# Conditioning sums of two segments moved from TensorE to GpSimd

## The chip, the cores and the metric

One core of one Trainium2 chip runs the kernel. The metric is the device time of one execution in microseconds, as the median of several. A core has five engines with queues of their own: TensorE (PE), VectorE (DVE), ScalarE (ACT), GpSimd (POOL) and SyncE (SP, which here issues DMAs). They are ordered against each other by semaphores alone.

## The reference, cut to what matters

Two decoder layers over 256 tokens of width 1024, the first with native sparse attention, the second with latent attention, each followed by a SwiGLU network. Each sub-layer is modulated by a conditioning vector:

```python
cond = jax.nn.silu(c)
for i in range(DEPTH):
    mod = cond @ ada_w[i] + ada_b[i]
    sh_m, sc_m, g_m, sh_f, sc_f, g_f = [t[:, None, :] for t in jnp.split(mod, 6, axis=-1)]
    hm = _rms(x, norm_mix[i]) * (1.0 + sc_m) + sh_m
    ...
    x = x + g_m * y.astype(x.dtype)
    hf = _rms(x, norm_ffn[i]) * (1.0 + sc_f) + sh_f
    x = x + g_f * _swiglu(hf, ffn_w_in[i], ffn_w_out[i])
```

Everything is float32. The twelve parts of `mod` (two layers, six each) are the segments 0 to 11. Segments 3 and 4 are `sh_f` and `sc_f` of the first layer. A segment is a product of the 1024 conditioning values with a 1024x1024 block of `ada_w`, plus a bias.

## The kernel before

**Weights.** All weights go through a ring. SP loads 1 MB at a time into `raw`; ACT copies half of it, a "slot" of 128x1024, rounded, into `w_hi` (line 776); DVE writes the rest, `raw - w_hi`, into `w_lo` (line 1121). PE multiplies each slot in three products (high by high, low by high, high by low; lines 1808 to 1810) into PSUM tensors `lin`. `w_hi` and `w_lo` have four slots, so ACT and DVE prepare a slot when PE has used the one four before it. A plain slot is 12 products of 512 columns, a slot of a compression unit 12 of 256.

**The first mixer.** After the first two input units (until about 59 us) PE goes through `U_KVW`, `U_QA`, the gates, the first compression `U_CMPK`, `U_QB` and the second compression `U_CMPV`, four slots each but for the gates. Between them stand transposes of what DVE has made from earlier units. DVE's program, an order written out by hand, is for this stretch: `w_lo` of the next slots; `normed_keys(0)` (sums of squares, a chain of ten small operations for reciprocal roots, two scalings L1390); `blocks(0)` (L1405); `normed_keys(1)`; `blocks_low` (`a_lo`, L1411); `blocks(1)`; `normed_queries(0)` (L1422, the same chain, L1426); `blocks_low`; `ada_biases(3)`; and, after the scaled copies of the queries, `normed_queries(1)`, `ada_biases(4)` and the compressed key. PE needs `a_lo` before each compression, the scaled keys before their transposes, and the second `normed_queries` before the last ones.

**Conditioning segments.** Segments 0 and 1 are done in the first 50 us. The weights of the others come as chunks of 128 rows by 1024 columns (512 KB), eight to a segment, through `ada_ring`, which has three places; POOL issues these loads (line 613) when a chunk three before is used. For segments 2 and 5 to 11 DVE adds each chunk, times its conditioning value, into `acc` (line 1205), and PE sums `acc` over the partitions at the end (`reduce_columns`, `reduce_row`). For segments 3 and 4 PE multiplies each chunk itself: after each slot of `U_KVW`, `U_QA`, `U_CMPK` and `U_QB` stands one `ada_chunk`, four fp32 matmuls of 32 by 256 (eight records in the profile) into `sc`. DVE then adds a bias into `ada_rows` (line 1214), PE turns that (`ada_turned`, line 1961), and `ada_columns` copies the result out.

**POOL** otherwise makes constants, issues small loads, zeroes and biases `acc` (line 683), adds steps of the first attention's output (line 703) and rotates the queries of the second (lines 440 to 447).

Of the kernel before, what the change touches and what calls it, by code (L numbers as in the profile page):

```python
# [17 lines left out]
F32 = mybir.dt.float32  # L18
# [49 lines left out]
BLOCKS = D // AQ  # L68

# [99 lines left out]
def rows_by_pe(seg):  # L169

    return sum(s not in VEC_SEGS for s in ADA_ORDER[:ADA_ORDER.index(seg)])


def chunks_by_pe(a):

    return sum(seg_at(n // KD) not in VEC_SEGS for n in range(EARLY * KD, a))
# [16 lines left out]
def trunk(nc, x_in, c_in, positions, ada_w, ada_b, norm_mix, norm_ffn, ffn_w_in, ffn_w_out,  # L193
# [4 lines left out]
    with ctx:  # L198
# [11 lines left out]
        ada_rows = sb("ada_rows", [P, 3, AQ], F32)  # L210
        ada_bias = sb("ada_bias", [P, 2, AQ], F32)
# [58 lines left out]
        with nsa:  # L270
# [12 lines left out]
            cstat = sb("cstat", [P, 3, H], F32, nsa)  # L283

# [58 lines left out]
        bias_zero = sem("bias_zero")  # L343
        bias_landed = [sem(f"bias_landed{n}") for n in range(2)]
        acc_bias = sem("acc_bias")
        ada_used = sem("ada_used")
        ada_biased = sem("ada_biased")
# [254 lines left out]
        def _(pool):  # L602
# [12 lines left out]
            def issue_bias(seg):  # L615
                layer, s6 = divmod(seg, 6)
                n = rows_by_pe(seg)
                if n >= 2:

                    pool.wait_ge(ada_biased, n - 1)  # L620
                for j in range(4):
                    c0 = s6 * D + AQ * j
                    pool.dma_start(ada_bias[32 * j:32 * j + 1, n % 2, :],
                                   ada_b[layer:layer + 1, c0:c0 + AQ]).then_inc(bias_landed[n % 2], 16)

# [3 lines left out]
            nc.gpsimd.memset(ada_bias[:], 0.0).then_inc(bias_zero, 1)  # L629
# [26 lines left out]
            pool.wait_ge(bias_zero, 1)  # L656
# [6 lines left out]
            def issue_next(a):  # L663

                if a + ARING < NSEG * KD:
                    if seg_at(a // KD) in VEC_SEGS:
                        pool.wait_ge(acc_summed, chunks_by_dve(a + 1))
                    else:
                        pool.wait_ge(ada_used, chunks_by_pe(a + 1))
                    issue(a + ARING)  # L670
# [18 lines left out]
            for seg in (3, 4):  # L689
                issue_bias(seg)  # L690
                supply(seg)
# [414 lines left out]
        def _(dve):  # L1106
# [102 lines left out]
            def ada_biases(seg):  # L1209

                n = rows_by_pe(seg)
                dve.wait_ge(ada_used, chunks_by_pe((place_of(seg) + 1) * KD))
                dve.wait_ge(bias_landed[n % 2], 64 * (n // 2 + 1))
                nc.vector.tensor_tensor(ada_rows[:, seg % 3, :], sc[place_of(seg) % 2][:, 0:AQ], ada_bias[:, n % 2, :],
                                        ALU.add).then_inc(ada_biased, 1)

            def ada_columns(seg):
                dve.wait_ge(ada_red, ada_at(seg))
                if seg in VEC_SEGS:
                    nc.vector.tensor_copy(ada_cols[:, seg, :], sc[seg % 2][:, 0:KD]).then_inc(ada_out, 1)  # L1220
                else:
                    nc.vector.tensor_copy(ada_cols[:, seg, :].rearrange("p (j h) -> p j h", h=2),
                                          sc[place_of(seg) % 2][:, 256:512].rearrange(
                                              "p (h j r) -> p j h r", h=2, r=32)[:, :, :, 0]).then_inc(ada_out, 1)
# [227 lines left out]
            ada_biases(3)  # L1452
# [7 lines left out]
            ada_biases(4)  # L1460
# [342 lines left out]
        def _(pe):  # L1803
# [53 lines left out]
            def unit(unit, s0, slots, n, lhs, wait_st=None, chunk_after=()):  # L1857
# [4 lines left out]
                for q, kts in enumerate(slots):  # L1862
# [12 lines left out]
                    if q in chunk_after:  # L1875
                        ada_chunk()
# [53 lines left out]
            def rows_product(seg, kt, chunk):  # L1930

                for j in range(4):
# [544 lines left out]
```

## Time and profile before

| | |
|---|---|
| median of 3 runs | 737.58 us (736.84 to 737.87) |
| the profiled execution | 737.94 us, span 736.1 us |
| PE busy | 699.7 us (95%) |
| DVE busy | 525.1 us (71%) |
| ACT busy | 373.4 us (51%) |
| POOL busy | 98.2 us (13%) |
| mean granted TensorE clock | 0.995 of full speed |

The span runs from the first to the last instruction; the execution's own time is 1.8 us longer. Busy times of PE count pipelined matmuls that overlap, so its pace is better read from the distance between their starts. Times of POOL are rougher than those of the others. "Idle before" is the time an engine stood still ahead of an instruction, with what released it.

### The profile page before, as it was taken

Reading aid. Unit: us, or ns where it says so; the run is one execution under the profiler, and the core shown is the slowest. Engines: PE = TensorE matmul, PEld = TensorE weight load, DVE = VectorE, ACT = ScalarE, POOL = GpSimd, SP = SyncE. Lnnn points to the kernel's source line nnn. Section 1 sums busy time; section 2 is a strip of 40 time slices with the busy share of each in tenths; the row PEclk is TensorE's granted clock in tenths of the full one; section 3 lists DMA queues with packets and bytes.
Section 4 is the critical chain, followed back from the end, with each engine's and each line's share of the span. In section 5 each row is a group of like instructions: output and inputs, shape, how many; then the busy total and the mean of one; then the engine's idle time right before and its main releaser. Section 6 shows DMA issues by size and latency. Waiting matters only on the chain. (4 is left out here: it accounts for less than half of the span.)

```text
span 736.1 us, 10780 instructions
## 1 busy us (share of the span) xinstructions
PE 699.7 (95%) x3903; PEld 575.5 (78%) x3903; DVE 525.1 (71%) x981; ACT 373.4 (51%) x696; POOL 98.2 (13%) x182
## 2 busy tenths in 40 slices
PE   3699999999989999999999999889999999999997
PEld 1577768888878888878878897778888888878886
DVE  3346687898888889887786578977767755554444
ACT  3244566577447444444333379676465444444341
POOL 7020212022110111221111100600001000000000
PEclk9999999999999999999999999999999999999999
DMA  8997996032248999997798372601538766554521
GB/s 289 351 371 187 372 369 228 2 116 86 90 170 262 334 326 354 321 342 273 265 341 289 94 211 66 228 1 59 172 111 276 230 189 193 171 173 171 204 83 57
DMA packets 93742, 155.09 MB, mean 211 GB/s; under 512 B 5979, under 2 KB 68064, under 8 KB 93696
## 3 DMA queue, kind: packets, MB, share of 16 engines
q1 hardware_dynamic: 80768, 111.24, 46.0%
q0 software_dynamic: 12928, 43.24, 17.3%
q8 instruction: 28, 0.46, 0.3%
q14 instruction: 18, 0.15, 0.1%
HBM read 151.32 MB, written 1.05 MB: 207 GB/s over the span
## 5 line engine op out<-in xcount | busy, mean ns | idle before, releaser
L776 ACT ACTIVATE w_hi<-raw 128x1024 fp32r<-128x1024 f32 (+3 forms) x198 | 201.5, 1024 | 263.2 <-PE lin L1810 238.3
L1121 DVE TENSOR_TENSOR w_lo<-raw,w_hi 128x1024 fp32r<-128x1024 f32 (+3 forms) x198 | 233.2, 1185 | 119.3 <-ACT w_hi L776 118.8
L1808 PE MATMUL lin<-w_hi,st_hi 128*128 128x512 f32 (+2 forms) x568 | 226.6, 399 | 2.3 <-DVE w_lo L1121 2.0
L1810 PE MATMUL lin<-w_hi,st_lo 128*128 128x512 f32 (+2 forms) x568 | 218.9, 385 | 0.0
L1809 PE MATMUL lin<-w_lo,st_hi 128*128 128x512 f32 (+2 forms) x568 | 218.6, 385 | 0.0
L1808 PEld LDWEIGHTS lin<-w_hi,st_hi 128*128 128x128 f32 x568 | 107.3, 189 | 28.1 <-issue 6.1
L1810 PEld LDWEIGHTS lin<-w_hi,st_lo 128*128 128x128 f32 x568 | 107.3, 189 | 21.3
L1809 PEld LDWEIGHTS lin<-w_lo,st_hi 128*128 128x128 f32 x568 | 107.6, 189 | 19.3 <-issue 0.7
L613 POOL DMA_DIRECT2D ada_ring<-in_ada_w_dram x80 | 42.7, 534 | 324.8 <-DVE acc L1205 238.7
L1205 DVE SCALAR_TENSOR_TENSOR acc<-ada_ring,cond_b,acc 128x1024 f32<-128x1024 f32 x64 | 81.8, 1279 | 3.3 <-DMA ada_ring<-in_ada_w_dram 3.1
L1808 PE MATMUL lin<-w_hi,hid_hi 128*128 128x512 f32 x176 | 70.1, 398 | 0.0
L1810 PE MATMUL lin<-w_hi,hid_lo 128*128 128x512 f32 x176 | 69.0, 392 | 0.0
L1809 PE MATMUL lin<-w_lo,hid_hi 128*128 128x512 f32 x176 | 68.5, 389 | 0.0
L1810 PEld LDWEIGHTS lin<-w_hi,hid_lo 128*128 128x128 f32 x176 | 33.0, 188 | 7.7
L1809 PEld LDWEIGHTS lin<-w_lo,hid_hi 128*128 128x128 f32 x176 | 33.1, 188 | 7.3 <-issue 0.2
L1808 PEld LDWEIGHTS lin<-w_hi,hid_hi 128*128 128x128 f32 x176 | 33.1, 188 | 6.8 <-issue 0.2
L848 ACT ACTIVATE z<-z,nmax 128x128 f32<-128x128 f32 x64 | 28.4, 445 | 11.6 <-DVE nmax L1279 11.6
L813 ACT ACTIVATE tfull<-tp,ada_cols,scale_cols 128x256 f32<-128x256 f32 x32 | 16.6, 558 | 13.9 <-issue 6.1
L1172 DVE TENSOR_TENSOR st_lo<-tfull,st_hi 128x512 fp32r<-128x512 f32 (+1 forms) x22 | 13.3, 607 | 12.8 <-ACT st_hi L816 12.6
L794 ACT ACTIVATE scratch<-x 128x512 f32<-128x512 f32 x16 | 10.0, 626 | 23.1 <-DVE x L1256 20.1
L1833 PE MATMUL tp<-ident,scratch 128*128 128x128 f32 x65 | 11.3, 299 | 10.9 <-DVE st_lo L1172 8.1
L1248 DVE TENSOR_TENSOR scratch<-lin,gate_rows 128x512 f32<-128x512 f32 x16 | 11.0, 687 | 11.3 <-PE lin L1810 11.3
(257 smaller groups left out, 858.1 us busy)
## 6 DMA issues: line engine op xcount, KB each, us to landing
raw<-in_ffn_w_in_dram SPq DMA_DIRECT2D x88, 512.0 KB, 5.2
ada_ring<-in_ada_w_dram POOLq DMA_DIRECT2D x80, 512.0 KB, 6.3
raw<-in_ffn_w_out_dram SPq DMA_DIRECT2D x22, 1024.0 KB, 6.1
raw<-in_nsa_w_in_dram SPq DMA_DIRECT2D x10, 1024.0 KB, 12.6
ada_first<-in_ada_w_dram SPq DMA_DIRECT2D x8, 1024.0 KB, 13.1
raw<-in_nsa_cmp_w_dram SPq DMA_DIRECT2D x4, 1024.0 KB, 9.9
raw<-in_nsa_w_out_dram SPq DMA_DIRECT2D x4, 1024.0 KB, 8.6
raw<-in_mla_w_out_dram SPq DMA_DIRECT2D x4, 1024.0 KB, 5.1
```

The source lines that it names most:

```text
L613: pool.dma_start(ada_ring[:, n % ARING, :], ada_source(a)).then_inc(ada_landed[n % ARING], 16)
L776: nc.scalar.activation(part_of(w_hi, s), raw_part(s), ACT.Copy).then_inc(hi_ready, 1)
L813: ins = nc.scalar.activation(dst, src, ACT.Identity, scale=scale[:, k:k + 1], bias=shift[:, k:k + 1])
L848: e = nc.scalar.activation(prob_b[:, n % 3, c0:c0 + w], prob_b[:, n % 3, c0:c0 + w], ACT.Exp, bias=nmax[:, n % 4, t:t + 1], scale=-1.0, ac ...
L1121: nc.vector.tensor_tensor(part_of(w_lo, s), raw_part(s), part_of(w_hi, s).bitcast(F32), ALU.subtract).then_inc(lo_ready, 1)
L1172: nc.vector.tensor_tensor(st_lo[:, k0:k0 + nk, :], tfull[:, m % 2, 0:nk * S].rearrange("p (k s) -> p k s", k=nk), st_hi[:, k0:k0 + nk, :]. ...
L1205: nc.vector.scalar_tensor_tensor(total, ada_ring[:, n % ARING, :], cond_b[:, kt, 0:1], total, ALU.mult, ALU.add).then_inc(acc_summed, 1)
L1248: ins = nc.vector.tensor_tensor(tmp, lin[2 * (unit % 2) + t][:], gate_rows[:, row, 512 * n:512 * n + 512], ALU.mult)
L1808: nc.tensor.matmul(bank, a_h, w_h, start=first, stop=False)
L1809: nc.tensor.matmul(bank, a_h, w_l, start=False, stop=False)
L1810: return nc.tensor.matmul(bank, a_l, w_h, start=False, stop=last)
L1833: ins = nc.tensor.transpose(tp[batch % 2][0:rows, n * P:(n + 1) * P], src, ident[:])
```

## The change

POOL gets two sums of its own, `shift_sum` and `scale_sum` (128x1024 each). At the start of its program it zeroes them and loads the bias into their first row. When the first chunks have landed it goes through the 16 chunks of segments 3 and 4: it multiplies the chunk in place by its conditioning value, waits for that, adds it to the sum, and waits for that before it issues the load of the chunk three further on. PE no longer has `ada_chunk` between its slots. Where `ada_turned` stood it now runs `reduce_columns` for both segments, which waits for POOL's sums and makes eight one-column products of each. DVE's two `ada_biases` go; `ada_columns` copies from the reduced columns. `ada_rows` shrinks, `ada_bias` and its loads go, and PE waits for the small loads explicitly in `compressed`.

```diff
 BLOCKS = D // AQ
+POOL_SEGS = (3, 4)
...
         ada_ring = sb("ada_ring", [P, ARING, D], F32)
-        ada_rows = sb("ada_rows", [P, 3, AQ], F32)
-        ada_bias = sb("ada_bias", [P, 2, AQ], F32)
+        scale_sum = sb("scale_sum", [P, D], F32)
+        ada_rows = sb("ada_rows", [P, 2, AQ], F32)
         x = sb("x", [P, T, D], F32)
...
             cstat = sb("cstat", [P, 3, H], F32, nsa)
+            shift_sum = sb("shift_sum", [P, D], F32, nsa)
+        pool_sums = {POOL_SEGS[0]: shift_sum, POOL_SEGS[1]: scale_sum}
...
-            def issue_bias(seg):
-                layer, s6 = divmod(seg, 6)
-                n = rows_by_pe(seg)
-                if n >= 2:
-
-                    pool.wait_ge(ada_biased, n - 1)
-                for j in range(4):
-                    c0 = s6 * D + AQ * j
-                    pool.dma_start(ada_bias[32 * j:32 * j + 1, n % 2, :],
-                                   ada_b[layer:layer + 1, c0:c0 + AQ]).then_inc(bias_landed[n % 2], 16)
-
             link(nc.gpsimd.memset(ident[:], 0.0))
             nc.gpsimd.affine_select(out=ident[:], in_=ident[:], compare_op=ALU.not_equal, fill=1.0, base=0,
                                     pattern=[[-1, P]], channel_multiplier=1).then_inc(ident_ready, 1)
-            nc.gpsimd.memset(ada_bias[:], 0.0).then_inc(bias_zero, 1)
+            for seg in POOL_SEGS:
+                link(nc.gpsimd.memset(pool_sums[seg][:], 0.0))
+                pool.dma_start(pool_sums[seg][0:1, :], ada_b[0:1, seg * D:(seg + 1) * D]).then_inc(sums_biased, 16)
             for n in range(ROT // 2):
...
                     pool.dma_start(dst, src).then_inc(small_in, 16)
-            pool.wait_ge(bias_zero, 1)
             pool.wait_ge(landed[2], 16)
...
                     else:
-                        pool.wait_ge(ada_used, chunks_by_pe(a + 1))
+                        pool.wait_ge(pool_summed, chunks_by_pool(a + 1))
                     issue(a + ARING)
...
-            for seg in (3, 4):
-                issue_bias(seg)
-                supply(seg)
+            def chunk_added(a):
+
+                place, kt = divmod(a, KD)
+                n = a - EARLY * KD
+                chunk = ada_ring[:, n % ARING, :]
+                total = pool_sums[seg_at(place)][:]
+                pool.wait_ge(ada_landed[n % ARING], 16 * (n // ARING + 1))
+                nc.gpsimd.tensor_scalar(chunk, chunk, cond_b[:, kt, 0:1], None, ALU.mult).then_inc(chunk_scaled, 1)
+                pool.wait_ge(chunk_scaled, n + 1)
+                if n > 0:
+                    pool.wait_ge(pool_summed, n)
+                nc.gpsimd.tensor_tensor(total, total, chunk, ALU.add).then_inc(pool_summed, 1)
+                issue_next(a)
+
+            pool.wait_ge(cond_ready, 1)
+            pool.wait_ge(sums_biased, 16 * len(POOL_SEGS))
+            for seg in POOL_SEGS:
+                for kt in range(KD):
+                    chunk_added(place_of(seg) * KD + kt)
...
-            def ada_biases(seg):
-
-                n = rows_by_pe(seg)
-                dve.wait_ge(ada_used, chunks_by_pe((place_of(seg) + 1) * KD))
-                dve.wait_ge(bias_landed[n % 2], 64 * (n // 2 + 1))
-                nc.vector.tensor_tensor(ada_rows[:, seg % 3, :], sc[place_of(seg) % 2][:, 0:AQ], ada_bias[:, n % 2, :],
-                                        ALU.add).then_inc(ada_biased, 1)
-
             def ada_columns(seg):
                 dve.wait_ge(ada_red, ada_at(seg))
-                if seg in VEC_SEGS:
-                    nc.vector.tensor_copy(ada_cols[:, seg, :], sc[seg % 2][:, 0:KD]).then_inc(ada_out, 1)
-                else:
-                    nc.vector.tensor_copy(ada_cols[:, seg, :].rearrange("p (j h) -> p j h", h=2),
-                                          sc[place_of(seg) % 2][:, 256:512].rearrange(
-                                              "p (h j r) -> p j h r", h=2, r=32)[:, :, :, 0]).then_inc(ada_out, 1)
+                nc.vector.tensor_copy(ada_cols[:, seg, :], sc[seg % 2][:, 0:KD]).then_inc(ada_out, 1)
...
             blocks_low()
-            ada_biases(3)
             low_to(CMPV0 + 3)
...
             normed_queries(1)
-            ada_biases(4)
...
                     ins.then_inc(slot_used, 1)
-                    if q in chunk_after:
-                        ada_chunk()
...
-            def rows_product(seg, kt, chunk):
-
-                for j in range(4):
-                    ins = nc.tensor.matmul(sc[place_of(seg) % 2][32 * j:32 * j + 32, 0:AQ], cond_b[:, kt, :],
-                                           chunk[:, AQ * j:AQ * j + AQ], start=(kt == 0), stop=(kt == KD - 1))
-                return ins
-
-            next_chunk = [EARLY * KD]
-
-            def ada_chunk():
-
-                a = next_chunk[0]
-                place, kt = divmod(a, KD)
-                seg = seg_at(place)
-                n = a - EARLY * KD
-                if kt == 0:
-
-                    if place == EARLY:
-                        pe.wait_ge(vec_ready, 1)
-                    else:
-                        pe.wait_ge(ada_biased, rows_by_pe(seg_at(place - 1)))
-                pe.wait_ge(ada_landed[n % ARING], 16 * (n // ARING + 1))
-                rows_product(seg, kt, ada_ring[:, n % ARING, :]).then_inc(ada_used, 1)
-                next_chunk[0] += 1
-                while next_chunk[0] < NSEG * KD and seg_at(next_chunk[0] // KD) in VEC_SEGS:
-                    next_chunk[0] += KD
-
-            def ada_turned(seg):
-
-                pe.wait_ge(ada_biased, rows_by_pe(seg) + 1)
-                for h in range(2):
-                    ins = nc.tensor.transpose(sc[place_of(seg) % 2][:, 256 + h * P:256 + (h + 1) * P],
-                                              ada_rows[:, seg % 3, h * P:(h + 1) * P], ident[:])
-                ins.then_inc(ada_red, 1)
-
             def wait_acc(seg):
...
-                wait_acc(seg)
-                total = acc[:, VEC_SEGS.index(seg) % 4, :]
+                if seg in POOL_SEGS:
+                    pe.wait_ge(pool_summed, KD * (POOL_SEGS.index(seg) + 1))
+                    total = pool_sums[seg][:]
+                else:
+                    wait_acc(seg)
+                    total = acc[:, VEC_SEGS.index(seg) % 4, :]
                 for k in range(KD):
...
-            unit(U_KVW, KVW0, FOUR, 512, stationary, latent_keys, EACH)
+            unit(U_KVW, KVW0, FOUR, 512, stationary, latent_keys)
...
+                pe.wait_ge(small_in, N_SMALL)
                 pe.wait_ge(*emptied(hidden_batch))
...
             transposed_keys(0)
-            unit(U_QA, QA0, FOUR, 512, stationary, None, EACH)
+            unit(U_QA, QA0, FOUR, 512, stationary)
             transposed_keys(1)
...
                     ins.then_inc(slot_used, 1)
-            compress(0, U_CMPK, CMPK0, None, EACH)
+            compress(0, U_CMPK, CMPK0)
             wait_tp(T_G)
             pe.wait_ge(unit_empty_act, U_GATE + 1)
             for t in range(T):
                 ins = nc.tensor.transpose(tp[T_G % 2][:, t * NG:(t + 1) * NG], gates_t[:, t * P:(t + 1) * P],
                                           ident[0:NG, 0:NG])
             ins.then_inc(tp_filled, 1)
-            unit(U_QB, QB0, FOUR, 512, stationary, None, EACH)
+            unit(U_QB, QB0, FOUR, 512, stationary)
             transposed_queries(0, T_QA)
...
             transposed_queries(1, T_QB)
-            ada_turned(3)
-            ada_turned(4)
+            reduce_columns(3)
+            reduce_columns(4)
             transposed_hidden(1, T_SCV)
```

## Rows read from the trace of the kernel before

**Rows 1.** The page's first part: busy time and share of each engine
```profile
PE 699.7 (95%) x3903; PEld 575.5 (78%) x3903; DVE 525.1 (71%) x981; ACT 373.4 (51%) x696; POOL 98.2 (13%) x182
```

**Rows 2.** Busy time by stretch: length, busy by engine, granted clock, DMA share, GB/s
```profile
55.00:124.20 69.20, 68.36 (x456) 50.95 (x454) 51.04 (x100) 39.46 (x55) 10.66 (x21) 1.00 0.92 305
55.00:111.40 56.40, 55.56 (x358) 40.24 (x357) 42.14 (x83) 31.94 (x44) 9.39 (x18) 1.00 0.93 310
```

**Rows 3.** Groups of DVE instructions by line and shape, 55 (last row: 50) to 124.1
```profile
L1121 DVE TENSOR_TENSOR w_lo<-raw,w_hi 128x1024 fp32r<-128x1024 f32 x20 | 23.9, 1217 | 11.7 <-ACT w_hi L776 11.6
L1411 DVE TENSOR_TENSOR a_lo<-scratch,a_hi 128x2048 fp32r<-128x2048 f32 x2 | 4.6, 2284 | 0.0
L1405 DVE TENSOR_TENSOR scratch<-z,vec_cols 128x120 f32<-128x120 f32 x16 | 4.5, 355 | 0.0
L1390 DVE TENSOR_TENSOR kdup_o<-proj,stat 128x512 f32<-128x512 f32 x4 | 2.6, 688 | 0.1
L1426 DVE TENSOR_TENSOR proj<-proj,stat 128x1024 f32<-128x1024 f32 x2 | 2.4, 1224 | 0.1
...
L1144 DVE TENSOR_TENSOR stat<-stat 128x16 f32<-128x16 f32 x2 | 0.4, 176 | 0.1
```

**Rows 4.** Timeline of PE between two slots (start us, us, instruction)
```profile
66.14 0.39 PE L1810 MATMUL lin<-w_hi,st_lo 128*128 128x512 f32 x1
...
67.36 0.39 PE L1809 MATMUL lin<-w_lo,st_hi 128*128 128x512 f32 x1
67.59 0.39 PE L1810 MATMUL lin<-w_hi,st_lo 128*128 128x512 f32 x1
```

**Rows 5.** Groups of PE instructions by line and shape, 59 to 126: the chunks
```profile
L1933 PE MATMUL sc<-ada_ring,cond_b 128*32 128x256 f32 x128 | 10.2, 391 | 0.8 <-DMA ada_ring<-in_ada_w_dram 0.8
```

**Rows 6.** Timeline of PE, at the old turning and at a reduction elsewhere
```profile
125.26 0.60 PE L1961 MATMUL sc<-ident,ada_rows 128*128 128x128 f32 x4
...
336.66 1.84 PE L1975 MATMUL sc<-ones,acc 128*128 128x1 f32 x16
338.36 0.48 PE L1808 MATMUL lin<-w_hi,st_hi 128*128 128x512 f32 x1
```

**Rows 7.** Groups of POOL instructions by line and shape, whole span
```profile
L703 POOL TENSOR_TENSOR kdup_o<-kdup_o,scratch 128x512 f32<-128x512 f32 x7 | 8.9, 1274 | 41.5 <-DVE scratch L1549 41.5
L683 POOL MEMSET acc<- 128x1024 f32 x8 | 7.7, 966 | 37.7 <-PE lin L1999 31.0 <-PE lin L1810 6.5
```

**Rows 8.** Timeline of DVE and POOL, 463 to 473
```profile
463.54 2.42 DVE L1121 TENSOR_TENSOR w_lo<-raw,w_hi 128x384 fp32r<-128x384 f32 x3
465.89 2.55 DVE L1723 TENSOR_TENSOR k_tok<-k_tok,stat 128x2048 f32<-128x2048 f32 x1
...
466.38 2.38 POOL L447 TENSOR_TENSOR q_tok<-scratch 128x128 f32<-128x128 f32 x1
...
472.44 0.46 POOL L447 TENSOR_TENSOR q_tok<-scratch 128x128 f32<-128x128 f32 x1
```

**Rows 9.** Timeline of POOL, first chunk loads and a memset's follower
```profile
41.97 1.64 POOL L613 DMA_DIRECT2D ada_ring<-in_ada_w_dram  x3 [26.39 <-DMA raw<-in_nsa_w_in_dram]
...
125.24 0.50 POOL L686 DMA_DIRECT2D acc<-in_ada_b_dram  x1 [0.29 <-POOL acc L683]
```

**Rows 10.** Timeline of DVE and POOL, 150 and 186 to 187
```profile
150.41 0.16 DVE L1542 SCALAR_TENSOR_TENSOR coef<-sums,gates 128x8 f32<-128x8 f32 x1
...
185.90 1.28 POOL L703 TENSOR_TENSOR kdup_o<-kdup_o,scratch 128x512 f32<-128x512 f32 x1 [3.98 <-DVE scratch L1549]
186.27 0.42 DVE L1572 TENSOR_TENSOR st_lo<-tp,st_hi 128x256 fp32r<-128x256 f32 x1 [0.18 <-ACT st_hi L834]
...
186.61 0.60 DVE L1542 SCALAR_TENSOR_TENSOR coef<-sums,gates 128x8 f32<-128x8 f32 x1
```

**Rows 11.** Busy time by stretch around 37 us, columns as in rows 2
```profile
34.00:37.30 3.30, 0.93 (x6) 0.86 (x6) 2.95 (x5) 2.41 (x4) 0.00 (x0) 0.92 1.10 356
37.40:40.80 3.40, 3.40 (x11) 2.66 (x10) 0.62 (x1) 0.00 (x0) 0.00 (x0) 0.59 1.03 408
```

More of the change, by code:

```diff
@@ L166, in seg_at, with chunks_by_pool @@
     return ADA_ORDER[place - EARLY]
[L169 to L176, printed above, removed]
+def chunks_by_pool(a):
+    return sum(seg_at(n // KD) in POOL_SEGS for n in range(EARLY * KD, a))
 def chunks_by_dve(a):
@@ L342, in trunk @@
         ident_ready = sem("ident_ready")
-        bias_zero = sem("bias_zero")
-        bias_landed = [sem(f"bias_landed{n}") for n in range(2)]
+        sums_biased = sem("sums_biased")
         acc_bias = sem("acc_bias")
-        ada_used = sem("ada_used")
-        ada_biased = sem("ada_biased")
+        chunk_scaled = sem("chunk_scaled")
+        pool_summed = sem("pool_summed")
         acc_summed = sem("acc_summed")
@@ L1855, in last_unit, with unit @@
                         ins.then_inc(part_done, 1)
-            def unit(unit, s0, slots, n, lhs, wait_st=None, chunk_after=()):
+            def unit(unit, s0, slots, n, lhs, wait_st=None):
                 wait_unit(unit)
@@ L2174, in _, with compress @@
             KT16 = [[0, 1, 2, 3], [4, 5, 6, 7], [8, 9, 10, 11], [12, 13, 14, 15]]
-            def compress(b, u, s0, among=None, chunk_after=()):
+            def compress(b, u, s0, among=None):
                 pe.wait_ge(a_ready, b + 1)
-                unit(u, s0, KT16, CH, lambda k: [(a_hi[:, k, :], a_lo[:, k, :])], among, chunk_after)
-            EACH = range(4)
+                unit(u, s0, KT16, CH, lambda k: [(a_hi[:, k, :], a_lo[:, k, :])], among)
             pe.wait_ge(consts, 1)
```

## The prediction

> **What bounds the kernel now.** I read the page's engine totals first. TensorE (PE) is busy for 95% of the span, VectorE (DVE) for 71%, GpSimd (POOL) for 13% [rows 1]. The change touches 55 to 126 us, so I cut that out next: from 55.0 to 124.2 us PE is busy for 68.36 of 69.20 us at full granted clock, and DVE for 51.04 [rows 2]. PE sets the pace here. DVE has 18 us of slack, most of it waits for ScalarE's `w_hi` (11.6 us) [rows 3]. The slack is uneven: from 55.0 to 111.4 DVE is busy for 42.14 of 56.40 us, and in this part it must finish all that PE's last compression unit needs. So two questions decide: what PE gets back, and whether DVE stays inside its slack once POOL computes beside it.
>
> **What PE gets back.** PE's timeline shows one slot's end and its chunk [rows 4]. The last weight product of a slot starts at 66.14, the second product of the next slot at 67.36, 1.22 us later, with the chunk and one product between them. The usual step is 0.23 (67.36 to 67.59), so two of them would have taken 0.46. A chunk costs PE 0.76 us; 128 records in eights are 16 chunks [rows 5], 12.2 us. PE's only wait for a chunk, 0.8 us [rows 5], lies where DVE will decide. Added to PE: the two transposes of `ada_turned`, 0.60 us for both segments, become two `reduce_columns`, each from 336.66 to 338.36 when it stands elsewhere, 1.70 us [rows 6]. So 3.4 less 0.6, +2.8 us, and nothing hides it: it stands in PE's queue ahead of filler matmuls and the transpose of the compressed key. If PE alone decided, the sum would be -12.2 + 2.8 = -9.4 us.
>
> **What POOL must do.** 16 times: a 128x1024 multiply, a wait on it, a 128x1024 add, a wait, the issue of the next chunk. A POOL add of 128x512 takes 1274 ns [rows 7], one of 128x128 takes 0.46 us undisturbed [rows 8]. That slope (0.81 us for 384 columns) gives 2.35 us for 1024; twice the 128x512 gives 2.55 as upper bound, 2.2 is the lower one if part of the small one's time is its strides. I take 2.33. No POOL multiply of one tensor is in the trace. From below stands a memset of the same size, 0.97 us [rows 7], which reads nothing; from above the add, 2.4. The multiply has one stream in and one out, the memset one out, the add two in over one read path; so it is nearest to the memset. I take 1.2 us and keep 1.0 and 2.4. From a POOL memset to the instruction that waits for it pass 0.29 us, and a DMA issue takes 0.50 to 0.55 [rows 9]: two waits and the issue are 1.1 us. Undisturbed, a chunk takes 1.2 + 2.33 + 1.1 = 4.6 us. The first three are issued from 41.97 [rows 9]; with 6 to 8 us to land POOL starts near 50 and would end at 50 + 16 x 4.6 = 124. PE, 12.2 us earlier than its 125.26 [rows 6], wants the second sum at 113. So even undisturbed the gain is nearly used up.
>
> The Trainium skill (GPSIMD Engine Reference, "When to use GPSIMD") calls one-input work on GpSimd roughly line rate. As an estimate from that page the multiply would be near 0.95 us instead of 1.2 and the total some 4 us lower; no multiply in the trace decides it.
>
> **What POOL does to DVE.** This is the larger term. At 463 to 469 us both engines work from SBUF [rows 8]. A POOL add that takes 0.46 us at 472.44 took 2.38 from 466.38 to 468.76: it ran only when DVE's product of two SBUF tensors had ended at 468.44. Three `w_lo` of 384 columns, some 0.5 us each by the 1217 ns for 1024 [rows 3], took 2.42 among POOL's adds. A DVE operation of 0.16 us at 150.41 took 0.60 at 186.61 and ended at 187.21, within 0.03 us of the end of POOL's 1.28 us add [rows 10]. Right before it DVE's `st_lo`, with one input in PSUM, ran beside the same add in 0.42, no longer than without. So an operation that reads two SBUF tensors and a POOL operation that reads SBUF exclude each other to the end of the instruction, less about 0.1 us.
>
> The Trainium skill (SBUF — State Buffer, "Who interferes with whom") has a rule that speaks against this change: a VectorE instruction with two SBUF inputs and a GpSimd instruction that reads SBUF block each other fully, whichever comes first. If they shared bandwidth instead, the total would be some 20 us lower. By that rule the row at 186.61 is the normal case, and the trace agrees.
>
> **How much of DVE's work is of this kind.** From 55 to 124 us: 20 `w_lo` (23.9 us), `a_lo` (4.6), the block sums L1405 (4.5), the scaled keys L1390 (2.6) and queries L1426 (2.4), and 28 operations of about 0.17 us, seven in each of four chains of reciprocal roots (4.8) [rows 3]. That is 42.8 of 51.04 us. POOL's chunks hold the port for 1.1 + 2.2 = 3.3 us each; 15 of the 16 lie behind 55 us: 49.5 us. With DVE's 42.8 that is 92 us of one port in a stretch that lasted 69, and would have to last 57 for the gain.
>
> **The sum.** DVE's program up to the end of the second `normed_queries` (124.2 us) becomes: start 55; work 51.04 less 0.42 for an `ada_biases`; 1.8 us of small gaps; about 4 us of waits that stay (for the transposed vectors and the first slots); and POOL's 49.5 us, less what falls on DVE's one-input work or waits. DVE does some 5.4 us of one-input work before POOL is through, and POOL holds the port for 3.3 us of a period of 5.7: 3 us; waits and late slots cover about 6. So 40.5 us stay. The end is 55 + 50.6 + 1.8 + 4 + 40.5 = 151.9 against 124.2: +27.7 us. POOL's own end: 4.6 us a chunk and twice some 0.55 of waiting for a DVE operation, 5.7 x 16 = 91, so 141; it isn't last. PE waits for DVE all the way: for the second batch of scaled keys, for `a_lo`, for `w_lo` of slots 24 to 26. With +2.8 for the reductions: +30.5. The profiled execution took 737.94 us, span 736.1; that gives 768.4 in its time, and the median of 737.58 lies 0.36 below: 768 us. What stands behind 130 us keeps its length.
>
> **Edits costed at nothing.** The two memsets and bias DMAs at POOL's start (2 x (0.97 + 0.3 + 0.5), less 0.5 for `ada_bias`) move POOL's constants and vector loads 3 us later; these are issued within the first 20 us and first needed near 59. Without that cover it would cost those 3 us. The eight bias DMAs that go, the `cond_ready` wait and PE's new `small_in` wait stand beside work long done. Chunk issues through POOL's queue come 5.7 instead of 3.5 us apart, which relieves DMA engines that are busy for 0.92 of the stretch [rows 2]; no engine waits for a weight there. Behind the waits of `chunk_added` POOL's queue holds only the next issues and the `acc` memsets, needed after the first attention begins.
>
> **Clock.** PE's granted clock fell to a mean of 0.59 of full speed from 37.4 to 40.8 us, after a stretch in which PE was busy for 0.93 of 3.3 us [rows 11]. The change makes PE idle for stretches like that. Where DVE decides it costs nothing; ahead of a PE-bound stretch, up to 3 us. I take nothing and keep 3 for the range.
>
> **Rivals.** (A) DVE goes first wherever both ask, and POOL alone is late. For it: DVE issues without a pause. Against it: the 2.42 us of three `w_lo`, among POOL's adds. Then POOL ends near 141 instead of 113 and PE waits for its second sum: 737.6 - 12.2 + 2.8 + 28 = 756. (B) The multiply costs as much as the add: 1.2 us more, 15 times, 18 us: 786. (C) No blocking at this size, POOL ends at 124, and PE's reduction stands where the old one stood: no change, 737. (D) The other side: DVE isn't blocked and POOL needs at most (113 - 50) / 16 = 3.95 us a chunk, waits included. Then the full -9.4: 728. Multiply, add and issue at their lower bounds make 3.7 us before any wait. The gain begins below 4.6 us a chunk.
>
> **Chances.** My forecast 0.68, with a range of its own of 756 to 780 (port held for 3.0 to 3.8 us a chunk, 5 to 12 us of overlap). A 0.12, B 0.09, C 0.04, D 0.07. The range for 8 in 10 reaches beyond A and nearly to B: 751 to 784. Slower by over 0.2%, about what this measurement can tell from no change: 0.89; within 0.2%: 0.03, as C seldom lands on exactly equal; faster: 0.08.
>
> **What would show it.** In the changed profile: POOL multiplies of about 1.2 us and adds of 2.33, many much longer where `w_lo` runs; `w_lo` with a mean well above 1.22 us and single ones of 3; POOL's last chunk near 141; DVE's second `normed_queries` ending near 152; PE some 60% busy from 70 to 150 us, waiting for `w_lo`, the keys and `a_lo`; `reduce_columns(4)` not waiting for POOL. The prediction is wrong if `w_lo` stays at 1.22 us (C or D), if PE's long wait is for the POOL sum (A), or if the multiply takes over 2 us (B).

## The result: 777.8 us, 5.5% slower

The changed kernel took 777.77 us (median of 4 runs, 776.55 to 778.49) against 737.21 for the kernel before in the same comparison (735.52 to 737.87). The ratio is 1.0553, 95% interval 1.0532 to 1.0574: 40.6 us more. The forecast of 768 was 9.8 us short; its range of 751 to 784 holds the time.

The page's totals of the changed kernel, answering to [rows 1]:

```profile
PE 701.7 (91%) x3803; PEld 585.8 (76%) x3803; DVE 555.2 (72%) x979; ACT 373.1 (48%) x696; POOL 192.8 (25%) x209
```

POOL has 94.6 us more work, DVE 30.1, and PE, with 100 matmuls fewer on record, is busy for 2.0 us more: what it saved came back as reductions and as matmuls at half clock. The busy time by stretch of the changed kernel, columns as in [rows 2]:

```profile
55.00:136.50 81.50, 60.82 (x322) 51.33 (x320) 77.31 (x99) 39.30 (x55) 76.47 (x36) 0.92 0.72 228
136.50:160.40 23.90, 4.90 (x25) 4.82 (x25) 5.39 (x16) 1.37 (x2) 22.45 (x11) 0.51 0.29 88
160.40:170.00 9.60, 9.60 (x55) 9.56 (x55) 2.03 (x9) 1.95 (x3) 3.54 (x5) 0.62 0.18 55
```

Three phases. Up to 136.5 DVE is busy for 77.31 of 81.50 us (51.04 in [rows 2]): it sets the pace. Then for 24 us hardly anyone but POOL works (PE for 4.90 us, DVE for 5.39). Then PE works at 0.62 of its clock. The groups of POOL and of DVE's `w_lo` in the changed kernel, against [rows 3] and [rows 7]:

```profile
L683 POOL TENSOR_SCALAR ada_ring<-ada_ring,cond_b 128x1024 f32<-128x1024 f32 x16 | 54.4, 3401 | 5.5 <-DMA ada_ring<-in_ada_w_dram 4.9
L687 POOL TENSOR_TENSOR shift_sum<-shift_sum,ada_ring 128x1024 f32<-128x1024 f32 x8 | 20.5, 2559 | 0.7
L687 POOL TENSOR_TENSOR scale_sum<-scale_sum,ada_ring 128x1024 f32<-128x1024 f32 x8 | 19.7, 2464 | 0.7
...
L1124 DVE TENSOR_TENSOR w_lo<-raw,w_hi 128x1024 fp32r<-128x1024 f32 x20 | 35.3, 1810 | 2.5 <-ACT w_hi L779 2.5
```

The multiply is POOL's longest work, at 3.4 us each and longer than the add. `w_lo` costs DVE 35.3 us instead of 23.9, and its slack (11.7 us of waiting for `w_hi`) has shrunk to 2.5. What PE waits for in the changed kernel, 55 to 170 us:

```profile
PE sc L1930 <- POOL scale_sum L687: 18.9, 1, 18.9
PE lin L1796 <- DVE w_lo L1124: 7.9, 4, 4.5
PE tp L1821 <- DVE proj L1416: 6.1, 2, 4.1
PE tp L1821 <- DVE kdup_o L1380: 5.1, 2, 4.0
```

The waits for DVE are the forecast's; the largest, for `scale_sum`, is rival A's mark. POOL's timeline of the changed kernel at its end, where nobody disturbs it:

```profile
148.84 2.85 POOL L683 TENSOR_SCALAR ada_ring<-ada_ring,cond_b 128x1024 f32<-128x1024 f32 x1
151.78 2.33 POOL L687 TENSOR_TENSOR scale_sum<-scale_sum,ada_ring 128x1024 f32<-128x1024 f32 x1
154.40 0.60 POOL L610 DMA_DIRECT2D ada_ring<-in_ada_w_dram  x1 [0.30 <-POOL scale_sum L687]
155.05 2.85 POOL L683 TENSOR_SCALAR ada_ring<-ada_ring,cond_b 128x1024 f32<-128x1024 f32 x1
```

A chunk takes 155.05 - 148.84 = 6.21 us with nothing in its way. PE's timeline of the changed kernel after DVE's second `normed_queries`:

```profile
136.60 1.67 PE L1821 MATMUL tp<-ident,proj 128*128 128x128 f32 x8 [4.07 <-DVE proj L1416]
138.06 3.41 PE L1930 MATMUL sc<-ones,shift_sum 128*128 128x1 f32 x16
160.37 3.57 PE L1930 MATMUL sc<-ones,scale_sum 128*128 128x1 f32 x16 [18.89 <-POOL scale_sum L687]
...
166.82 0.42 PE L1821 MATMUL tp<-ident,scratch 128*128 128x128 f32 x1
```

The last row is the transpose of the compressed key, the step that lets attention begin. The kernel before reached it at 127.65, so it is 39.2 us late, the whole loss: the two profiled executions lie 38.6 us apart (spans of 774.7 and 736.1). It divides into 12.3 us (the transposes of the second queries begin at 136.60 instead of 124.30), 18.9 us for POOL's sum, 6.4 us (reductions of 3.41 and 3.57 us where two transposes took 0.60, [rows 6]) and 1.6 us for the query transposes and filler matmuls around them, at half clock.

### The profile page after: what moved, and what is told of

Read it like the earlier page. It is cut to its first block and busy times, and to the rows that moved or that the text cites. A ratio compares the mean times of both kernels' runs of the same rounds, so it can differ in the third digit from the quotient of the medians.

```text
span 774.7 us, 10617 instructions
## 1 busy us (share of the span) xinstructions
PE 701.7 (91%) x3803; PEld 585.8 (76%) x3803; DVE 555.2 (72%) x979; ACT 373.1 (48%) x696; POOL 192.8 (25%) x209
## 5 line engine op out<-in xcount | busy, mean ns | idle before, releaser
L1124 DVE TENSOR_TENSOR w_lo<-raw,w_hi 128x1024 fp32r<-128x1024 f32 (+3 forms) x198 | 246.7, 1256 | 110.1 <-ACT w_hi L779 109.7
L683 POOL TENSOR_SCALAR ada_ring<-ada_ring,cond_b 128x1024 f32<-128x1024 f32 x16 | 54.4, 3401 | 5.5 <-DMA ada_ring<-in_ada_w_dram 4.9
L1930 PE MATMUL sc<-ones,scale_sum 128*128 128x1 f32 x16 | 3.6, 353 | 18.9 <-POOL scale_sum L687 18.9
## 6 DMA issues: line engine op xcount, KB each, us to landing
raw<-in_nsa_w_in_dram SPq DMA_DIRECT2D x10, 1024.0 KB, 11.7
ada_first<-in_ada_w_dram SPq DMA_DIRECT2D x8, 1024.0 KB, 13.1
```

Source lines behind the costliest of these rows:

```text
L683: nc.gpsimd.tensor_scalar(chunk, chunk, cond_b[:, kt, 0:1], None, ALU.mult).then_inc(chunk_scaled, 1)
L1124: nc.vector.tensor_tensor(part_of(w_lo, s), raw_part(s), part_of(w_hi, s).bitcast(F32), ALU.subtract).then_inc(lo_ready, 1)
```

## Experiments

Each kernel but that of experiment 12 is the changed one with the edit shown. The kernel before stood at 736.5, 736.9 and 737.2 us in the three groups of comparisons. Two marks of the traces are given with the times: Q, when PE begins the transposes of the second queries (124.30 before, 136.60 changed), and R, when it begins the `sc<-acc,ones` row reduction behind the first attention (204.06 before, 243.48 changed).

### 1. PE doesn't wait for POOL

```diff
-    ins = matmul(sc[...], total[:, k * P:(k + 1) * P], ones[:, 0:1])    # segments 3 and 4
+    ins = matmul(sc[...], ident[:], ones[:, 0:1])
```

> The changed kernel, but the two reductions of segments 3 and 4 multiply the identity instead of POOL's sums and wait for nothing of POOL (this leaves the conditioning of segments 3 and 4 out of the result). Theory P (POOL's chain of 16 chunks is what ends last, since its multiply takes 2.85 us and not 1.2): the 18.9 us wait of PE goes, DVE's program keeps its delay of 12 us at the second normed_queries, and the time falls to 755 to 760 us. Theory V (as predicted: DVE, kept from its port, ends last, and the wait for POOL only covers it): POOL's wait goes but PE waits for DVE instead, and the time stays above 766 us.

Measured: 760.65 us, ratio 1.0358 [1.0302, 1.0414]; Q 136.53, R 227.26. This is theory P, 0.7 us beyond its upper end. 17.1 of the 40.6 us are PE's wait for the sum, near the trace's 18.9. The other 23 are there without it.

### 2 to 4. POOL's arithmetic left out, all or in part

```diff
-    tensor_scalar(chunk, chunk, cond_b[:, kt, 0:1], None, ALU.mult)     # out in 2 and 3
-    tensor_tensor(total, total, chunk, ALU.add)                         # out in 2 and 4
```

> The changed kernel, with POOL doing neither multiply nor add (the chunks are loaded but not summed, which leaves them out of the result); PE's work is that of the changed kernel. It prices what PE gets back: with the chunk matmuls gone and nobody in DVE's way. Prediction's terms: -12.2 + 2.8 = -9.4, so 728 us. Rival: DVE has no slack in this stage even undisturbed, then only a part comes, 732 to 737 us.

> The changed kernel, without POOL's multiply (unscaled chunks are summed, which leaves the conditioning values out). POOL's chunk becomes one add of 2.33 us, a wait and an issue, 3.3 us and what it waits for the port; it ends near 110 us and PE doesn't wait for it. Theory: what is left over the run without POOL arithmetic is DVE's blocking by adds: 16 x 2.2 us of port, some 15 to 20 us of it on DVE's path, so 742 to 750 us. Rival (blocking costs little, the delay of DVE comes from the multiplies): under 735 us.

> The changed kernel, without POOL's add (the chunks are scaled and not summed, which leaves them out). POOL's chunk is one multiply of 2.85 us, a wait and an issue, 3.8 us; POOL ends near 112. In the changed kernel small DVE operations on two SBUF tensors ran freely in the later part of a multiply, so I think that the multiply holds the port for its first 1.1 us only: then 16 x 1.1 us, 8 to 10 of it on DVE's path, 735 to 741 us. Rival (it holds the port for all of its 2.85 us, more than the add): as slow as the run with adds only or slower, over 745 us.

| kernel | us | ratio | Q | mean `w_lo`, ns |
|---|---|---|---|---|
| 2, neither | 739.98 | 1.0051 [1.0037, 1.0065] | 119.56 | 1219 |
| 4, multiply alone | 740.7 | 1.0061 [1.0037, 1.0085] | 122.85 | 1463 |
| 3, add alone | 760.92 | 1.0333 [1.0301, 1.0365] | 140.54 | 1966 |
| changed kernel | 777.77 | 1.0553 [1.0532, 1.0574] | 136.60 | 1810 |

Two misses. With no arithmetic on POOL nothing was gained (728, or 732 to 737, expected), though 12.2 us of products were gone. And the adds alone cost more than the 742 to 750 expected: Q is 21.0 us later than in kernel 2 (140.54 less 119.56). With the multiplies alone it is 3.3 later, and the median only 0.7 us higher (the profiled execution of kernel 4, 742.77 us, lies 2.1 above its median). Groups of POOL and DVE in the kernel with multiplies alone:

```profile
L683 POOL TENSOR_SCALAR ada_ring<-ada_ring,cond_b 128x1024 f32<-128x1024 f32 x16 | 54.9, 3433 | 5.6 <-DMA ada_ring<-in_ada_w_dram 5.0
...
L1120 DVE TENSOR_TENSOR w_lo<-raw,w_hi 128x1024 fp32r<-128x1024 f32 x22 | 31.3, 1463 | 1.7 <-ACT w_hi L775 1.7
```

POOL is busy for 54.9 us beside DVE and delays it little: a long instruction isn't a long hold. But Q alone doesn't price the hold, as DVE's waits cover part of it. Busy time from 48 us to Q, columns as in [rows 2], of kernels 2, 4, 3 and the changed one:

```profile
48.00:119.56 71.56, 65.71 (x357) 56.20 (x355) 53.09 (x105) 43.87 (x61) 10.22 (x19) 0.95 0.97 331
48.00:122.85 74.85, 65.24 (x356) 54.96 (x354) 66.28 (x105) 43.77 (x61) 66.17 (x35) 0.98 0.94 308
48.00:140.54 92.54, 70.16 (x357) 58.57 (x355) 87.70 (x105) 43.97 (x61) 51.72 (x35) 0.87 0.79 255
48.00:136.60 88.60, 67.75 (x355) 56.81 (x353) 81.70 (x105) 43.80 (x61) 81.34 (x37) 0.92 0.74 237
```

The same 105 DVE instructions take 13.2 us longer beside 16 multiplies (66.28 less 53.09), 0.8 us each, and 34.6 us longer beside 16 adds, 2.2 us each. Of the 13.2 us, 9.9 go into time in which DVE stood idle in kernel 2 (18.5 us there, 8.6 here); part of that idle time is kernel 2's own trouble with its loads, which comes next. In the changed kernel DVE's instructions are 28.6 us longer. It reaches Q earlier than the one with adds alone because only 12 of its 16 chunks were through by then, where all 16 adds were: the multiply, by its length, spreads the adds out.

### 5 to 7. Where the 12.2 us of PE went

```diff
@@ 5 and 7: issue(a), segments 3 and 4
-    dma_start(ada_ring[:, n % ARING, :], ada_source(a))
+    dma_start(ada_ring[:, n % ARING, 0:8], ada_source(a)[:, 0:8])
@@ 6 and 7: both behind the first attention, before unit(U_OUT0, ...)
+    reduce_columns(3)
+    reduce_columns(4)
```

All three leave POOL's arithmetic out as kernel 2 does. Where the reductions move, DVE's two `ada_columns` move with them, and PE's wait for these ahead of the first attention goes.

> POOL leaves out the multiplies and adds of segments 3 and 4, and loads only 8 of the 1024 columns of each of their chunks (so their values are wrong); the reductions stand in their old place. With full loads it took 740.0, although PE does 12.2 us less of chunk products. Theory: the loads, no longer held back by PE's use of the chunks, take DMA time from the weights and the spread of the keys, and PE waits for those; without them PE gets some 7 us more: 731 to 734. Rival: DVE's own work is the bound once PE has no chunks: 738 to 740.

> POOL leaves out the multiplies and adds of segments 3 and 4 (their values are wrong by that), and the reductions stand behind the first attention. The same kernel with the reductions in their old place took 740.0. If those reductions cost 5.5 us there and 3.4 us later: 737 to 738. If they also caused the half clock that followed (3 us more of fillers and transposes at half speed): 735. Rival: the half clock comes from PE's waits before them, so it stays: 738 or more.

> As the kernel with small loads and no arithmetic on POOL, and with the reductions behind the first attention: what the change could give if POOL's work cost nothing and nothing stood in the way. All of the 12.2 us less 3.4 for the reductions, +0.6 for what they replace: 728. If DVE or the clock bound it: 733 to 737.

| kernel | us | ratio | Q | R |
|---|---|---|---|---|
| 2, full loads, old place | 739.98 | 1.0051 [1.0037, 1.0065] | 119.56 | 206.73 |
| 5, small loads | 733.31 | 0.9946 [0.9931, 0.9961] | 112.78 | 200.04 |
| 6, late reductions | 739.77 | 1.0049 [1.0026, 1.0072] | 119.27 | 206.88 |
| 7, both | 733.13 | 0.9952 [0.9931, 0.9972] | 113.43 | 199.68 |

The loads are 6.7 us, as the theory of kernel 5 had it; the theories of kernels 6 and 7 failed (735 to 738 and 728 expected) and their rivals held. DMA issues from 50 to 126 us (size, median us from issue to landing), first kernel 2, then kernel 5:

```profile
raw<-in_nsa_cmp_w_dram SPq DMA_DIRECT2D x4, 1024.0 KB, 13.6
...
raw<-in_nsa_w_in_dram SPq DMA_DIRECT2D x3, 1024.0 KB, 13.3
```

```profile
raw<-in_nsa_cmp_w_dram SPq DMA_DIRECT2D x4, 1024.0 KB, 8.7
...
raw<-in_nsa_w_in_dram SPq DMA_DIRECT2D x3, 1024.0 KB, 5.4
```

Without PE's pace to hold them back, the chunk loads ran as fast as the ring allowed, and the weights of these two groups took 5 to 8 us longer (those of a third, `in_nsa_w_out_dram`, 5.8 and 5.7 us, did not). In kernel 2 ACT waits 6.0 us for landed weights, in kernel 5 not at all. With small loads Q comes at 112.78, 11.5 us before that of the kernel before: the 12.2 us of chunk products were real. But R comes only 4.0 earlier. Moving the reductions changed neither time. PE's timeline of kernel 7 shows why:

```profile
175.17 1.90 PE L1927 MATMUL sc<-ones,shift_sum 128*128 128x1 f32 x16
176.93 3.28 PE L1927 MATMUL sc<-ones,scale_sum 128*128 128x1 f32 x16
180.81 0.78 PE L1793 MATMUL lin<-w_hi,st_hi 128*128 128x512 f32 x1
181.38 0.63 PE L1794 MATMUL lin<-w_lo,st_hi 128*128 128x512 f32 x1
...
184.91 0.40 PE L1793 MATMUL lin<-w_hi,st_hi 128*128 128x512 f32 x1
```

The second reduction takes 3.28 us where the first took 1.90, and the weight products behind it 0.63 instead of 0.40 (0.78 for the first). PE never stopped: the stretch is fully busy and the granted clock is half, 1.2 GHz. The stretches before the first reduction and from the second on, in kernel 7:

```profile
165.00:175.10 10.10, 9.89 (x91) 8.99 (x90) 7.88 (x28) 7.07 (x28) 2.15 (x4) 1.00 0.19 54
...
176.90:184.00 7.10, 7.10 (x31) 6.41 (x31) 1.56 (x3) 0.60 (x1) 0.00 (x0) 0.52 0.00 0
```

The Trainium skill (TensorE: Matmul & The Clock Gate, "What's actually happening") says that the clock follows how busy PE has been, and gives idle time as the reason for a fall. Here it fell in a stretch without idle time, of two reductions of one-column matmuls; by idle time alone kernel 7 would have kept the full clock.

### 8. The reductions apart

```diff
+    def among_output(k):
+        wait_low(k)
+        if k in (2, 6):
+            reduce_columns(3 if k == 2 else 4)
-    unit(U_OUT0, OUT0, FOUR, 512, stationary, st_wait(T_O0, nsa_outputs))
+    unit(U_OUT0, OUT0, FOUR, 512, stationary, among_output)
```

> POOL leaves out the multiplies and adds of segments 3 and 4 and loads 8 of 1024 columns of their chunks (their values are wrong); the two reductions stand in the first output unit, 1.3 of its 4 slots from each other, not one behind the other. With both together the second ran at half clock, at either place, and the weight products behind it too until some 10 us had passed; that took back 7 of the 11 us that the kernel had gained by its first attention. If the pair in a row is the cause: no half clock there, 726 to 727. If any one-column reduction at this place lowers the clock, or the clock falls for another reason: 731 or more.

Measured: 730.37 us, ratio 0.9910 [0.9879, 0.9941]; Q 111.92 and R 196.20. PE's timeline of this kernel:

```profile
178.92 1.84 PE L1927 MATMUL sc<-ones,shift_sum 128*128 128x1 f32 x16
186.19 1.84 PE L1927 MATMUL sc<-ones,scale_sum 128*128 128x1 f32 x16
```

Both run at full clock, and no half clock follows (1.00 throughout 165 to 190 us). The time lies between the two forecasts. R is 3.5 us earlier than in kernel 7, where the last product of the attention stood 0.4 later, so 3.1 are gained behind it. The medians' intervals overlap, so it is the trace that shows this gain, not the times. Of the 7 us that I had put down to the clock only these 3.1 are the clock's; the rest is the reductions themselves, 1.7 us each at full clock. The edit does two things: it parts the reductions, and it puts the first among weight products instead of directly behind the attention's small ones. No run here tells these apart. R is 7.9 us earlier than in the kernel before, near the -9.4 of the prediction's sum for PE. This is what the change could have given had POOL's work and its loads been free.

### 9 and 10. The whole computation, with the reductions late

The changed kernel in full, the two reductions behind the first attention, in a row (9, the edit of 6) or apart (10, that of 8).

> The changed kernel with the reductions of segments 3 and 4, and DVE's copies of them, moved behind the first attention, where their values are first needed; the same result is computed. If PE's long wait in the changed kernel is only its place in PE's queue ahead of the compressed key (theory: POOL's sum is late, the reductions stand too early), the wait of 18.9 us goes and so do the 6.8 us that the reductions took at half clock, and 3.4 us come back later: about 757, and no PE instruction waits for POOL. POOL still multiplies and adds until 160, beside the first attention, and DVE's second normed queries still end near 136.5. Rival: what is lost is lost to DVE's port alone and the wait only hides it: no better than 772.

> The changed kernel in full, with the same result, its two reductions in the first output unit and apart from each other. With both in a row in front of that unit it took 762.5. If the half clock behind the pair costs it 7 us there too: 755 to 756; what then remains over the kernel before is the port: DVE's second normed queries 12 us later, and POOL's last four chunks beside the first attention. If the clock isn't it: 761 to 763.

Measured: 762.48 us, 1.0359 [1.0306, 1.0412], R 228.71; and 759.52 us, 1.0341 [1.0276, 1.0407], R 225.56. Q is 136.50 and 136.47. Kernel 9 is 5 us above its forecast but far below the rival's 772, and PE no longer waits for POOL in either; kernel 10 lies between its two forecasts. Moving the wait away gains what leaving it out gained (15 and 17 us), and setting the reductions apart 3.2 us more at R. Both do everything that the changed kernel does, and both stay over 3% slower than the kernel before. Between kernels 8 and 10, 730.4 and 759.5, stand 29 us for POOL's arithmetic and its full loads.

### 11. A shorter multiply

```diff
-    tensor_scalar(chunk, chunk, cond_b[:, kt, 0:1], None, ALU.mult)
+    tensor_tensor(chunk, chunk, cond_b[:, kt, 0:1].broadcast_to([P, D]), ALU.mult)
```

> The changed kernel, but POOL multiplies each chunk as a product of two tensors, the column repeated over the 1024 elements. The same result. Alone this instruction took 1.89 us, the multiply by a column 2.82. If POOL's own length alone sets its end, each of the 16 chunks is 0.95 us shorter: POOL's last add ends near 145 instead of 160 and the kernel takes about 763. But the multiply by a column lets DVE through after its first part (in the run of single instructions seven 128x1024 DVE adds fitted beside some three multiplies), and the product of two tensors should hold the port to its end as the add does. Then DVE loses about 1 us more a chunk, its second normed queries end near 146 instead of 136.5, and POOL's end moves only to 155 or so: 771 to 775.

Measured: 786.87 us, 1.0667 [1.0646, 1.0688]. Groups of POOL and `w_lo`, PE's longest wait, DVE's second `normed_queries` and the busy time from 48 us to Q in this kernel:

```profile
L683 POOL TENSOR_TENSOR ada_ring<-ada_ring,cond_b 128x1024 f32<-128x1024 f32 x16 | 32.0, 1999 | 5.0 <-DMA ada_ring<-in_ada_w_dram 4.8
...
L1125 DVE TENSOR_TENSOR w_lo<-raw,w_hi 128x1024 fp32r<-128x1024 f32 x21 | 49.3, 2401 | 0.0
...
PE tp L1822 <- DVE kdup_o L1381: 33.6, 2, 20.5
...
164.70 1.23 DVE L1417 TENSOR_TENSOR proj<-proj,stat 128x1024 f32<-128x1024 f32 x1
...
48.00:165.98 117.98, 71.63 (x355) 58.74 (x353) 113.82 (x105) 44.19 (x61) 87.69 (x51) 0.81 0.62 200
```

POOL's multiplies are 22 us shorter in all and its last add ends at 141.1, where the prediction had it for the changed kernel, and yet the kernel is 9 us slower. DVE's second queries now end at 165.9, 29.4 us later than in the changed kernel. I had expected DVE to be later by 10 us, a third of it, and the kernel at 771 to 775, faster than the changed one: a miss. The rows show where it comes from. DVE's 105 instructions take 60.7 us longer than in kernel 2 (113.82 less 53.09), 3.8 a chunk where the changed kernel has 2.4 (28.6 over 12 chunks), and all 16 chunks fall ahead of Q instead of 12. PE waits for DVE and no longer for POOL: this kernel shows the mechanism that I predicted for the changed one, with a higher price.

### 12. Single instructions

> No part of the reference is computed: POOL and DVE run rows of single instructions on constant tiles. First POOL alone, four of each: multiply by a column, by a constant, copy, add, multiply of two tensors (128x1024), then narrower ones. Then four POOL instructions of 128x1024 beside a row of short DVE instructions of 128x128, which show when DVE is let through. Theory: multiply by a column 2.85 us, add 2.33; a copy or a multiply by a constant near 1.2 if it is the column that makes it slow, near 2.85 if it is the operation. Beside two-tensor DVE work the add holds the port to its end, so no DVE instruction ends during it; the multiply holds it only for its first 1.1 us, and some ten DVE instructions run within the rest of each. Rival: the multiply holds it to its end too, and what ran beside it in the changed kernel was luck of the order. One-input DVE instructions are held as well if the one of 1.63 us in the changed kernel was held; else not.

POOL alone, four of each (L213 multiplies by a column, L216 by a constant, L219 adds, L222 multiplies two tensors, L225 copies):

```profile
L213 POOL TENSOR_SCALAR pool_out<-a,c 128x1024 f32<-128x1024 f32 x4 | 11.3, 2842 | 11.8 <-DVE wide_out L255 11.8
L216 POOL TENSOR_SCALAR pool_out<-a 128x1024 f32<-128x1024 f32 x4 | 11.0, 2767 | 0.1
L219 POOL TENSOR_TENSOR pool_out<-a,b 128x1024 f32<-128x1024 f32 x4 | 9.2, 2337 | 0.1
L222 POOL TENSOR_TENSOR pool_out<-a,c 128x1024 f32<-128x1024 f32 x4 | 7.4, 1892 | 0.1
...
L225 POOL COPY pool_out<-a 128x1024 f32<-128x1024 f32 x4 | 4.0, 1039 | 0.1
```

It is the operation and not the column: a multiply by a constant takes 2.77 us, a copy 1.04. The Trainium skill (GPSIMD Engine Reference, "4.1 Engine selection"), whose figure the prediction drew on too, calls one-input work roughly line rate: the copy agrees, the multiply takes 2.7 times as long.

Beside DVE's rows: the first window is four POOL adds beside 128x1024 DVE adds, the second four POOL multiplies by a column beside the same (DVE, then POOL busy time):

```profile
294.26:307.29 13.03, 13.03 (x5) 13.03 (x4) 1.00 0.00 0
...
312.07:327.05 14.98, 9.45 (x7) 14.98 (x4) 1.00 0.00 0
```

Beside the adds five DVE instructions touch 13.03 us, one for each add: 2.3 us of POOL and 1.0 of DVE by turns, so the hold lasts to the add's end. Beside the multiplies DVE is through with its seven 128x1024 adds in 9.45 us, 1.35 each instead of 1.22. The mean hides who pays. DVE's timeline, one add beside a POOL add and one beside a POOL multiply:

```profile
295.17 3.36 DVE L219 TENSOR_TENSOR wide_out<-a,b 128x1024 f32<-128x1024 f32 x1
...
314.08 2.06 DVE L219 TENSOR_TENSOR wide_out<-a,b 128x1024 f32<-128x1024 f32 x1
```

A POOL add costs the DVE add that meets it 2.14 us (3.36 less 1.22), a POOL multiply 0.84, though it is the longer instruction. That is what kernels 3 and 4 lost for each, 2.2 and 0.8. What the theory said of the multiply, a hold of some 1.1 us at its start, holds for these. The theory failed for short DVE instructions. DVE's timeline of 96 adds of 128x128, and POOL's first multiply beside them:

```profile
71.09 19.49 DVE L219 TENSOR_TENSOR probe_out<-a,b 128x128 f32<-128x128 f32 x96 [58.91 <-POOL pool_out L219]
...
72.77 20.52 POOL L213 TENSOR_SCALAR pool_out<-a,c 128x1024 f32<-128x1024 f32 x1 [1.79 <-DVE probe_out L219]
```

DVE wasn't held at all: POOL's multiply waited until the row was over (71.09 + 19.49 = 90.58), and then took its 2.8 us. So did its first copy (18.7 us) and add (20.0 us). DVE's one-input copies and multiplies by a constant shut POOL out in the same way, for 13.1 us. DVE's multiplies by a column let POOL in, and then POOL's four adds kept DVE out (five DVE instructions in 9.4 us). Only DVE adds with one input in PSUM let both run: POOL's four adds took 9.26 us beside 49 of them.

The Trainium skill (SBUF — State Buffer, "Who interferes with whom") has it that issue order decides who blocks, and that a copy or `tensor_scalar` on DVE can take the shared ports as well, while one SBUF input otherwise doesn't. These rows agree with the last two. They disagree with "for the whole instruction" where POOL multiplies by a scalar (0.84 us lost beside 2.84), and issue order doesn't explain the row of 128x128 adds: POOL's multiply starts at 72.77 and waits for all the DVE adds that start after it, until 90.58.

## Why the prediction held, and where it was off

The time lies in the range, and the mechanism forecast (POOL keeps DVE from its SBUF operands, PE waits for DVE) is there. But two of the prediction's own signs of being wrong came true as well: PE's longest wait is for the POOL sum, and the multiply takes over 2 us. The near hit of the sum is partly luck, as shown below.

**What PE gets back** (-12.2 + 2.8 = -9.4) was right as a term: Q was 11.5 us earlier with POOL's work and loads away, R 7.9 us earlier with the reductions apart (kernel 8). I had not weighed the loads, and the clock at nothing. I wrote that later chunk issues relieve the DMA engines. In the changed kernel they did, as POOL was slow (DMA share 0.72 up to 136.5), and no engine there waits for a weight to land; the 6.7 us of kernel 2 are a cost of kernels without arithmetic.

**What POOL must do** had the mis-sized term that cost most. The add was right (2.33), the waits and the issue too. The multiply, taken at 1.2 from the memset with 2.4 as its upper end, takes 2.85: 4.6 + 1.65 = 6.25 us a chunk, and the trace has 6.21. With DVE's share 16 chunks took (160.3 - 50.1) / 16 = 6.9 us each, not 5.7, so POOL ended at 160.3, not 141, and `reduce_columns(4)` waited for it. The nearest row gave the wrong neighbour: a memset has no arithmetic.

**What POOL does to DVE.** The mechanism is shown: `w_lo` at 1810 ns on average, exclusion to the end of an add (experiment 12), 77 of 81.5 us busy. Its size was too large: +12.3 at Q instead of +27.7. The term is the 40.5 us of port time on DVE's way; the trace has 77.31 - 50.6 = 26.7. It is the count of chunks that was off, and with it again the slow multiply: only 11 of the 15 chunks behind 55 us were through by Q, and 11 at the forecast's 3.3, less its 9 us of cover, are 27.3. The price of a chunk was about right: 2.14 + 0.84 = 3.0 us in experiment 12, 2.2 + 0.8 in kernels 3 and 4, where I had 3.3. Where a shorter multiply takes its place and every POOL instruction holds the port, DVE loses far more (experiment 11).

**The sum.** Forecast +30.5 (27.7 and 2.8). The trace has 12.3 + 18.9 + 6.4 + 1.6 = 39.2. DVE's delay was 15.4 us too large, the wait for POOL, taken at nothing, 18.9 too small, and these two cancel but for 3.5 us. Reductions and clock add the other 5.2 (8.0 instead of 2.8), 8.7 us in all. The two large errors have one source, POOL's slower chunk: it relieves DVE and makes PE wait. Rivals A (PE waits for the sum) and B (a dear multiply) are each partly true, and neither with the forecast's mechanism gone: two paths set the end one after the other.

**Clock** at nothing was wrong. Of the 6.4 us, 3.0 would remain at full clock (twice 1.8 less 0.6), so 3.4 are the clock's, and with the 1.6 around the reductions it costs 5.0. I had allowed up to 3. Kernels 7 and 8 show that a stall isn't even needed for it.

Still open: why DVE's short instructions keep POOL out while 128x1024 ones take turns with it, and whether it is the second reduction or the place of the first that lowers the clock in kernel 7. Neither was taken further.

## What to carry to other kernels

In these runs work moved to GpSimd was paid for by VectorE where both worked from SBUF, and the price followed how long each GpSimd instruction held the port (2.1 us of an add of 2.3, 0.8 of a multiply of 2.8), not how long it ran: price both, and for every operation from a row of that operation. Put what consumes such work where its value is first needed: in a queue ahead of unrelated work a late sum holds up all of it (18.9 us here). Keep reductions of one-column matmuls apart from each other, among wide products (3.1 us here). And price a hold by the longer busy time of the engine that is held, not by the end of the stage alone: idle time of that engine hides it.

## What was unexpected of the hardware

- A GpSimd multiply of 128x1024 by a column or a constant takes 2.84 or 2.77 us, more than an add of two such tensors (2.34) or their product (1.89), and lets VectorE through for most of its length: a VectorE add of 1.22 us took 2.06 beside it, and 3.36 beside a GpSimd add.
- Back-to-back VectorE instructions of 128x128 kept a GpSimd instruction waiting for some 18 us and lost nothing themselves; with adds of 128x1024 on both, the two engines took turns.
- The TensorE clock fell to half after a reduction of 16 one-column matmuls when a second came directly behind it, with PE busy all the time, and came back some 7 us later (176.9 to 184 us); with both among weight products and 7 us from each other it stayed at 1.00.
